# Merged slots for the mixer's gelu-gate and short-convolution columns and for the up projection

## The reference, cut to what matters

```
def hybrid_mixer(u, ...):                       # in each of 2 layers, after a SwiGLU part, before another
    proj = u @ w_in                             # 1024 -> 14 x 1024
    xa, ya, q, k, v, g, sb, sc, sh, gates = jnp.split(proj, cuts, axis=-1)
    xa = causal_depthwise_conv(xa, lru_conv_w) + lru_conv_b
    ha = rg_lru(xa, ...)                        # a gated linear recurrence over the tokens
    oa = (ha * jax.nn.gelu(ya)) @ w_lru_out
    ...
    oc = (sb * causal_depthwise_conv(sc * sh, sc_conv_w)) @ w_sc_out
    ga, gb, gc = jnp.split(jax.nn.sigmoid(gates), 3, axis=-1)
    return (ga * oa + gb * ob + gc * oc) @ w_out

def second_block(...):
    ...
    a = jax.nn.relu(v_ @ w_up)                  # 1024 -> 4096
    ff = (a * a) @ w_down                       # 4096 -> 1024
```

## Time and profile before

| | us |
|---|---|
| median of 3 runs | 2032.05 (2031.1 to 2034.25) |
| the profiled execution | 2034.39 |
| its span | 2032.2 |
| TensorE busy | 1994.3 (98%) |
| VectorE busy | 1299.5 (64%) |
| ScalarE busy | 983.2 (48%) |

### The profile page before, as it was taken

The page is one execution under the profiler, slowest core; times in us unless marked ns, Lnnn a source line. Parts: engine busy times, 40 slices in busy tenths (PEclk is TensorE's granted clock), DMA queues, the critical chain, the costliest instruction groups (busy, mean ns, idle before and its releaser), DMA issues.

```text
span 2032.2 us, 27980 instructions
## 1 busy us (share of the span) xinstructions
PE 1994.3 (98%) x11612; PEld 1748.8 (86%) x11612; DVE 1299.5 (64%) x1601; ACT 983.2 (48%) x1358; POOL 102.9 (5%) x211
## 2 busy tenths in 40 slices
PE   9999999999999999999999999999999999999996
PEld 7888998879898888888889987888888888889985
DVE  7656777546556674766569754465667566766555
ACT  5445465354434544544455644543454445754443
POOL 1003000000000000100300000000010001010000
PEclk9999999999999999999999999999999999999999
DMA  7656456535656556565554464455655656345661
GB/s 252 203 186 212 131 187 202 192 125 167 205 188 207 166 187 201 172 206 187 191 193 165 150 224 149 163 186 187 207 168 187 228 184 194 119 156 188 186 208 61
DMA packets 245148, 369.31 MB, mean 182 GB/s; under 512 B 6679, under 2 KB 180023, under 8 KB 245022
## 3 DMA queue, kind: packets, MB, share of 16 engines
q1 hardware_dynamic: 240000, 352.34, 52.7%
q0 software_dynamic: 4528, 14.85, 2.2%
q10 hardware_dynamic: 494, 0.32, 0.1%
HBM read 366.28 MB, written 1.08 MB: 181 GB/s over the span
## 4 chain that ended last, share of the span: by engine, by line
PE 89%; DVE 5%; ACT 2%; DMA 1%; issue 1%; POOL 1%; DVEq 0%; SPq 0%; POOLq 0%; ACTq 0%
PE ps L1741 19%; PE ps L1551 19%; PE ps L1534 14%; PE ps L1535 7%; PE ps L1522 6%; PE ps L1524 6%; PE ps L1523 6%; PE ps L1612 4%; PE ps L1576 1%; DMA raw<-in_ffn_w_in_dram 1%; DVE w_lo L1016 1%; PE ps L1685 1%; DVE u L1066 1%; DVE a L1171 1%; PE ps L1896 1%
## 5 line engine op out<-in xcount | busy, mean ns | idle before, releaser
L1016 DVE TENSOR_TENSOR w_lo<-raw,w_hi 128x1024 fp32r<-128x1024 f32 (+1 forms) x658 | 765.5, 1207 | 366.5 <-ACT w_hi L658 364.7
L658 ACT ACTIVATE w_hi<-raw 128x1024 fp32r<-128x1024 f32 (+1 forms) x658 | 653.1, 1042 | 392.3 <-PE ps L1551 196.1
L1534 PE MATMUL ps<-u,w_hi 128*128 128x512 f32 x1280 | 451.1, 397 | 0.3 <-DVE act L1125 0.3
L1535 PE MATMUL ps<-u,w_lo 128*128 128x256 f32 x1280 | 359.2, 281 | 0.0
L1522 PE MATMUL ps<-u,w_hi 128*128 128x256 f32 x1072 | 306.5, 286 | 0.1
L1524 PE MATMUL ps<-u,w_lo 128*128 128x256 f32 x1072 | 303.3, 283 | 0.0
L1523 PE MATMUL ps<-u,w_hi 128*128 128x256 f32 x1072 | 303.3, 283 | 0.0
L1534 PEld LDWEIGHTS ps<-u,w_hi 128*128 128x128 f32 x1280 | 240.2, 188 | 59.0 <-issue 0.8
L1535 PEld LDWEIGHTS ps<-u,w_lo 128*128 128x128 f32 x1280 | 241.8, 189 | 0.2
L1741 PE MATMUL ps<-w_hi,u 128*128 128x512 f32 x640 | 205.4, 396 | 2.0 <-DVE w_lo L1016 2.0
L1522 PEld LDWEIGHTS ps<-u,w_hi 128*128 128x128 f32 x1072 | 205.6, 192 | 1.4 <-issue 0.8
(11 more groups left out here) (279 smaller groups left out, 2517.0 us busy)
## 6 DMA issues: line engine op xcount, KB each, us to landing
raw<-in_w_mix_in_dram SPq DMA_DIRECT2D x112, 1024.0 KB, 5.1
raw<-in_ffn_w_in_dram SPq DMA_DIRECT2D x88, 1024.0 KB, 5.1
raw<-in_ffn_w_out_dram SPq DMA_DIRECT2D x40, 1024.0 KB, 4.9
raw<-in_w_ret_out_dram SPq DMA_DIRECT2D x16, 1024.0 KB, 5.0
raw<-in_w_up_dram SPq DMA_DIRECT2D x16, 1024.0 KB, 5.5
raw<-in_w_down_dram SPq DMA_DIRECT2D x16, 1024.0 KB, 4.9
raw<-in_w_in_dram SPq DMA_DIRECT2D x9, 1024.0 KB, 5.3
raw<-in_w_lru_out_dram SPq DMA_DIRECT2D x8, 1024.0 KB, 5.0
```

Source lines behind the costliest of these rows:

```text
L658: A(parts(n)[0][:, part], raw[i % RAW][:, part], ACT.Copy).then_inc(heads_done, 1)
L1016: V.tensor_tensor(parts(n)[1][:, part], raw[i % RAW][:, part], parts(n)[0][:, part], ALU.subtract)\
L1534: M(ps[:, bank0 + a, :], hi[:, k, c], u[:, :, k, :], start=k == 0, stop=False)
L1535: ins = M(ps[:, bank0 + a, 0:S], lo[:, k, c], u_hi[:, k, :], start=False, stop=k == KD - 1)
```

## The change

The column slots of ya, sc, sh and sb in both layers and those of the up projection (but not its head slots) become wide slots. Each then fills two banks: bank pair (2+2j) mod 4 in the mixer, 2(p mod 2) in the up projection, so two results can wait instead of four. ScalarE copies the half with `hi*lo` into an SBUF tile, and VectorE adds the half from PSUM to it. What used the bank now uses the sum. For ya there is one tile for the sum, `act2[:, 1]`, so ScalarE copies ya j only after Gelu of ya j-1. In the up projection Relu is no longer taken by ScalarE; VectorE's square becomes max(x, 0) * x. TensorE waits for the add (`col_summed`, `relu_summed`) where it waited for the reader of the bank. The two head slots of the up projection are turned back into banks 4 and 5 instead of 1 and 2.

```diff
+WIDE = ("ya", "sc", "sh", "sb")
...
+        def col_halves(j):
+            return wide_halves((2 + 2 * j) % 4)
+        def col_sum(j):
+            return act2[:, j % 2, :].rearrange("p (a n) -> p a n", a=2)
... ScalarE, mixer
                         elif name == "ya":
-                            A(tiles(a2)[:, pair, :], pv, ACT.Gelu_apprx_tanh).then_inc(gelu_ready.sem, 1)
+                            if j >= 1:
+                                act.wait_ge(gelu_ready.sem, gelu_ready.at(l, j))
+                            A(col_sum(1), col_halves(j)[1], ACT.Copy).then_inc(col_low.sem, 1)
+                            act.wait_ge(col_summed.sem, col_summed.at(l, col_index(name, j) + 1))
+                            A(tiles(a2)[:, pair, :], col_sum(1), ACT.Gelu_apprx_tanh).then_inc(gelu_ready.sem, 1)
...
                         elif name == "sc":
-                            A(tiles(a1)[:, pair, :], pv, ACT.Copy).then_inc(sc_ready.sem, 1)
+                            A(tiles(a1)[:, pair, :], col_halves(j)[1], ACT.Copy).then_inc(col_low.sem, 1)
+                        elif name in ("sh", "sb"):
+                            if j >= 2:
+                                used = sh_ready if name == "sh" else oc_ready
+                                act.wait_ge(used.sem, used.at(l, j - 1))
+                            A(col_sum(j), col_halves(j)[1], ACT.Copy).then_inc(col_low.sem, 1)
... ScalarE, up projection
-                        A(act2[:, p % 2, :], ps[:, (9 + p) % 4, :], ACT.Relu).then_inc(b["relu_ready"], 1)
+                        if p < 2:
+                            A(act2[:, p % 2, :], ps[:, 4 + p, :], ACT.Copy).then_inc(b["relu_low"], 1)
+                        else:
+                            A(act2[:, p % 2, :].rearrange("p (a n) -> p a n", a=2), wide_halves(2 * (p % 2))[1], ACT.Copy)\
+                             .then_inc(b["relu_low"], 1)
... VectorE, mixer, after ahead(n) and ahead of the recurrence
+                        if name in WIDE:
+                            i = col_index(name, j)
+                            part = tiles(a1)[:, pair, :] if name == "sc" else col_sum(1 if name == "ya" else j)
+                            dve.wait_ge(col_low.sem, col_low.at(l, i + 1))
+                            V.tensor_tensor(part, col_halves(j)[0], part, ALU.add).then_inc(col_summed.sem, 1)
...
-                            V.tensor_tensor(prod_pad[:, pair, 2:2 + S], pv, tiles(a1)[:, pair, :], ALU.mult)\
+                            V.tensor_tensor(prod_pad[:, pair, 2:2 + S], col_sum(j), tiles(a1)[:, pair, :], ALU.mult)\
...
-                            own.done(V.tensor_tensor(tiles(a1)[:, pair, :], pv, tiles(a1)[:, pair, :], ALU.mult))
+                            own.done(V.tensor_tensor(tiles(a1)[:, pair, :], col_sum(j), tiles(a1)[:, pair, :], ALU.mult))
... VectorE, up projection
-                        V.tensor_tensor(mul2[:, p % 2, :], act2[:, p % 2, :], act2[:, p % 2, :], ALU.mult)\
-                         .then_inc(b["sq_ready"], 1)
+                        if p < 2:
+                            dve.sem_inc(b["relu_summed"], 1)
+                        else:
+                            low = act2[:, p % 2, :].rearrange("p (a n) -> p a n", a=2)
+                            V.tensor_tensor(low, wide_halves(2 * (p % 2))[0], low, ALU.add).then_inc(b["relu_summed"], 1)
+                            dve.wait_ge(b["relu_summed"], p + 1)
+                        V.scalar_tensor_tensor(mul2[:, p % 2, :], act2[:, p % 2, :], 0.0, act2[:, p % 2, :], ALU.max,
+                                               ALU.mult).then_inc(b["sq_ready"], 1)
... TensorE, mixer
-                            if name == "sc":
-                                pe.wait_ge(g_ready.sem, g_ready.at(l, j + 5))
+                            if name in WIDE and j >= 2:
+                                emptied_columns(l, name, j - 2)
+                            elif name in WIDE and BEFORE[name] in WIDE:
+                                emptied_columns(l, BEFORE[name], j + 2)
+                            elif name == "sc":
+                                pe.wait_ge(g_ready.sem, g_ready.at(l, 2 * j + 6))
+                            elif name in WIDE:
+                                before = EMPTIED[BEFORE[name]]
+                                pe.wait_ge(before.sem, before.at(l, 2 * j + 2))
...
-                            column_slot(n, bank((2 + j) % 4), u_hi, u_lo)
+                            if name in WIDE:
+                                wide_slot(n, (2 + 2 * j) % 4)
+                            else:
+                                column_slot(n, bank((2 + j) % 4), u_hi, u_lo)
... TensorE, up projection
-                    if p >= 4:
-                        pe.wait_ge(b["relu_ready"], p - 3)
                     if n not in HEADSLOT:
-                        column_slot(n, bank((9 + p) % 4), u_hi, u_lo)
+                        if p >= 4:
+                            pe.wait_ge(b["relu_summed"], p - 1)
+                        wide_slot(n, 2 * (p % 2))
                     if p == 2:
-                        turn_back(G_UP, (1, 2))
+                        turn_back(G_UP, (4, 5))
```

More of the change, by code:

```diff
@@ L272, in half_view, with col_index @@
             return [a.rearrange("p (k n) -> p k n", n=512) for a in parts(n)]
+        def col_index(name, j):
+            return 4 * WIDE.index(name) + j
+        def col_halves(j):
+            return wide_halves((2 + 2 * j) % 4)
+        def col_sum(j):
+            return act2[:, j % 2, :].rearrange("p (a n) -> p a n", a=2)
         def half_bank(e, tt):
@@ L346, in build @@
         ret_ready = signal("ret_ready", HEADS, 1)
-        sc_ready = signal("sc_ready", 4)
+        col_low = signal("col_low", 4 * len(WIDE))
+        col_summed = signal("col_summed", 4 * len(WIDE))
         sh_ready = signal("sh_ready", 4)
@@ L369, in build @@
             "attn_rows", "attn_sum", "attn_scale", "attn_scaled", "o_turned", "o_head", "o_ready",
-            "relu_ready", "sq_ready", "hid_ready", "p_loaded",
+            "relu_low", "relu_summed", "sq_ready", "hid_ready", "p_loaded",
             "p_turned", "p_head", "p_ready", "brow_loaded", "gate_rows", "gate_in", "gate_ready", "gated", "ple_sum",
@@ L825, in mixer @@
                         ahead(n)
-                        if name in ("xa", "ya", "sc") or name in ("ga", "g", "gb", "gc") and j % 2 == 1:
+                        if name in ("xa", "ya", "sc", "sh", "sb") or name in ("ga", "g", "gb", "gc") and j % 2 == 1:
                             emptied(n)
@@ L1289, in mixer @@
                         elif name == "sb":
-                            dve.wait_ge(slot_used, n + 1)
-                            own.done(V.tensor_tensor(tiles(a1)[:, pair, :], pv, tiles(a1)[:, pair, :], ALU.mult))
+                            dve.wait_ge(col_summed.sem, col_summed.at(l, i + 1))
+                            own.done(V.tensor_tensor(tiles(a1)[:, pair, :], col_sum(j), tiles(a1)[:, pair, :], ALU.mult))
                             split(tiles(a1)[:, pair, :], h_hi[:, pair, :], h_lo[:, pair, :], oc_ready.sem)
@@ L1447, in _ @@
                         p = 8 * part + j
[L1448 to L1450 removed]
+                        dve.wait_ge(b["relu_low"], p + 1)
+                        if p < 2:
[6 more added lines that the diff above has]
+                                               ALU.mult).then_inc(b["sq_ready"], 1)
                         dve.wait_ge(b["sq_ready"], p + 1)
@@ L1723, in turn_head, with emptied_columns @@
                 ins.then_inc(ret_turned.sem, 1)
[L1726 to L1729, removed]
+            EMPTIED = {"xa": xa_ready, "q": q_ready, "k": k_ready, "ga": ga_ready, "lru_out": acc_ready,
+                       "gb": gb_ready, "ret_out": ret_added, "gc": gc_ready}
+            BEFORE = {"q": "xa", "k": "q", "ya": "k", "ga": "ya", "lru_out": "ga", "g": "lru_out", "sc": "g",
                       "sh": "sc", "gb": "sh", "ret_out": "gb", "sb": "ret_out", "gc": "sb", "sc_out": "gc"}
+            def emptied_columns(l, name, j):
+                pe.wait_ge(col_summed.sem, col_summed.at(l, col_index(name, j) + 1))
             def half_slot(n, k0, act_hi, act_lo, e, first, last):
@@ L1762, in row_form @@
                     else:
-                        before = EMPTIED[BEFORE[name]]
-                        pe.wait_ge(before.sem, before.at(l, 2 * e + 2))
+                        if BEFORE[name] in WIDE:
+                            emptied_columns(l, BEFORE[name], 2 + e)
+                        else:
+                            before = EMPTIED[BEFORE[name]]
+                            pe.wait_ge(before.sem, before.at(l, 2 * e + 2))
                 if name == "lru_out" and j == 0:
@@ L1992, in _ @@
                     if n == B_DN2 + 4:
-                        pe.wait_ge(b["relu_ready"], 16)
+                        pe.wait_ge(b["relu_summed"], 16)
                         pe.wait_ge(b["p_loaded"], 16)
```

3 lines of the change are left out of this document (1 added, 2 removed).

## The result

| | us |
|---|---|
| the changed kernel, median of 8 runs | 2037.89 (2036.90 to 2039.18) |
| the kernel before, median of 8 runs | 2032.90 (2031.10 to 2034.25) |
| ratio, with its 95% interval | 1.0023 [1.0013, 1.0034] |
| the profiled execution and its span | 2036.92, 2035.1 |

It is slower, by 4.7 us (2.6 to 6.9, by the ratio). The forecast was 2036.4, and +4.3.

The account below looks back on a forecast made before the run. TensorE, computing 98% of the span, was taken as the bound. Slips at ya of +9.3 us less 5.0 saved in merged slots gave +4.3, median 2032.05 to 2036.4; range 2033.4 to 2039.8.

Parts of the forecast that it names:

- The slip at ya: ya0 to ya3: ScalarE's copies, loads and waits for adds delay recurrence and ga1 by 4.67 us a layer, +9.3 together.
- One small wait: At ya3, TensorE waiting for the sum of ya1 (302.74 against 302.72) costs nothing, since slot 18 waits anyway.
- The load has no drain: ScalarE's table loads at ya: 1.28 us uncovered, without the skill page's 1.38 drain, which would add 2.8.
- No slack behind 310.34: VectorE from the first layer's recurrence start: no pause, so any delay there delays ga1 at 337.20 equally.
- The gain elsewhere: 38 merged slots in sc, sh, sb and up save 5.0 us; 1.5 by the skill page's figures.
- all nineteen quick: sc1 to sh3 in both layers and up 3 to 7 all at quick pace: 1.9 us beyond 4.1.
- Nothing elsewhere: sc, sh, sb and up: copies and adds make TensorE wait nowhere; cover 1.2 us at gb2, 0.4 at up's entry.
- The sum: Whole kernel: +9.3 - 5.0 = +4.3 us, median 2032.05 becomes 2036.4.
- The forecast's edge of 4.06 us: Whole kernel: 0.2%, about what a measurement can tell from none; slower by more than that had chance 0.51.
- A: All 38 merged slots outside ya: quick pace everywhere, 7.8 us gained, +1.5, 2033.6; chance 0.12.
- B: ya0 to ya3: the recurrence doesn't slip, ScalarE's added waits lie in time it has, -5.0, 2027.1; chance 0.06.
- C: sh or the entry of up: VectorE falls behind by more than 1.2 us of cover, +7.3, 2039.4; chance 0.15.

Follow-up runs that it names:

- experiment 1: Changed kernel with ya put back to column slots, Gelu straight from the bank; sc, sh, sb and up stay merged: 2028.72 us, 0.9968 of the kernel before.
- experiment 2: Kernel before with only ya merged into wide slots: 2044.25 us, 1.0041 of the kernel before.
- experiment 5: Changed kernel plus a one-column Gelu ahead of the wait for ya0, to preload Gelu's table: 2036.49 us, 1.0011 of the kernel before.
- experiment 6: Changed kernel with VectorE's add of ya3 moved behind the first recurrence step: 2041.47 us, 1.0035 of the kernel before.
- experiment 3: Changed kernel with Exp and Sqrt ahead of all Gelus, each Gelu one slot later, ya3's add behind the first recurrence step: 2025.60 us, 0.9952 of before.
- experiment 4: Changed kernel with ya in column slots, Exp and Sqrt ahead of all Gelus, each Gelu one slot later: 2026.91 us, 0.9958 of the kernel before.
- experiment 7: Changed kernel with eight small matmuls, results overwritten, ahead of sb0 in both layers and of the second up half: 2042.91 us, one run.

## Why the prediction was right, point by point

- **The slip at ya.** Right, step by step. On the clock of before the forecast had the Gelu of ya0 at 293.54, the head of slot 15 at 298.67, that of 16 at 303.23, that of 17 at 311.06 and the recurrence at 315.01. The profile after has, with 1.86 added, 293.45, 298.61, 303.22, 311.06 and 315.01. ga1 was to slip 4.67 a layer and slipped 4.68 and 4.67; the waits were to be "some 12 us" and are 10.6. By start times the eight waits cost 12.7. Experiments 1 and 2 put all of it on ya, 5 and 6 show that it is a queue's order and not the table load alone. One small wait was put at nothing and did show: TensorE starts ya3 0.26 late, for the sum of ya1. As the prediction said, the waits behind it swallow it: in experiment 5 it is gone, and the slip is still 4.1.
- **The load has no drain.** Load and function start 1.29 apart here too (290.30, 291.59). The term that ScalarE: Activation LUTs, in the Trainium skill, section What ACT_TABLE_LOAD costs, would have added is not seen.
- **No slack behind 310.34.** Right for later starts: what came late there came out at ga1. Experiments 3 and 4 show the other direction, which the forecast didn't price: a start 1.85 earlier shortened the stretch by 1.31, and one 3.6 earlier by 1.33. That is the wait of before by start times, and with it gone an earlier recurrence is worth nothing.
- **The gain elsewhere.** The step "I take half of that: gain 5.0" was too low. It is the one term of the sum that was mis-sized. In the profile after all nineteen slots behind a turn were quick: 2.01 in each mixer (135.28 less 133.27) and 2.01 in up, together 6.03, where all nineteen quick had been reckoned at 4.1 + 1.9. The half came from two quick runs behind a turn "and not in a third"; the trace of before has four such runs, two quick (thirteen slots from 683.80, seven from 1518.87) and two slow (from 35.64 and from 872.07), so that the evidence was even. Of these the fourteen in sc and sh were quick in every profile of merged ones, the five of up in five of seven (5.668 in experiments 5 and 7). The figures of TensorE: Matmul & The Clock Gate, in the Trainium skill, section Back-to-back issue gap, by which the gain was estimated at 1.5, are off by four times here.
- **Nothing elsewhere.** Right. The first half of gb2's split was to be done 1.3 ahead of TensorE: it is done at 516.82 (the splits start at 515.60, 1.22 each), and gb2 starts at 518.17 (507.27 and two row slots of 5.45). At the entry of up the add of p2 ends at 1834.19 and TensorE takes p4 at 1834.53, a cover of 0.34 where 0.4 was forecast.
- **The sum.** 9.36 less 6.03 is +3.3, a microsecond under the forecast's +4.3, and that microsecond is the gain. The spans differ by 2.9, because the stretches that weren't changed differ too: -1.86 up to ya, and +1.37 in the second feed-forward part. The timed difference, +4.7 (2.6 to 6.9), holds both +3.3 and +4.3, so the times alone don't check the sum to a microsecond. That the medians lie +5.0 apart, within 0.7 of the forecast, is partly luck: the gain was put 1.0 too low, and the 1.7 between +3.3 and +5.0 is in no stretch that changed; one run of unchanged slots can move the time by 1.37. The rest of the miss is that the median of before went from 2032.05 to 2032.90 with more runs. The forecast's edge of 4.06 us lies inside the interval too, so on which side of it the change fell is not settled.
- **Rivals.** A (quick everywhere): sb and the second up half stayed at 5.65 in every run (5.67 and 5.66 behind the small matmuls). B (no slip): the slip is there; but experiments 3 and 4 are B made true, by another order, at -9.8 and -8.5. C (VectorE behind in sh): no wait at gb2.

## What to carry to other kernels

A saving on the engine that bounds a kernel counts only where that engine doesn't already wait; first look at which queue its last wait comes from, and whether the new helper work (a copy, a wait for an add, a table load) enters that queue ahead of the instruction that the wait is for. Here 6.0 us were won on TensorE in 38 slots and 9.4 lost in ScalarE's order at eight, and another order of the same work, with two table loads a layer less, won the loss back and a wait of the old kernel too. In a kernel like this one, try a result's last step behind the next slot's weight preparation where it has to wait for another engine (experiment 6 shows what one such wait ahead of it costs), and group functions that share a table.

## What the runs showed of the hardware

A merged pair (512 and 256 moving columns) has two paces, 5.65 and 5.55 us per 16 pairs, 353 and 347 ns a pair. The granted clock is 1.00, the 2.4 GHz level, in both (684 to 756 before, quick; 1900 to 1945 in the profile after, slow). The quick pace is what the other forms' spacings add up to, an estimate from their rows: 5.45 / 24 = 0.227 for 512 columns and 5.759 / 48 = 0.120 for 256. The slow one has 6 ns more a pair.

A run keeps its pace from its second or third slot to its end, and which one it is changes between executions of the same instructions. In the first feed-forward part, where nothing was changed, thirteen slots took 5.697 us each in the profile before, 5.599 in the one after and 5.659 in experiment 4. These are averages with the first slots in them: before it is 6.12, 5.75 and then 5.65; after, 6.12, 5.66 and then 5.55; in experiment 4, 5.73 and then 5.65. The thirteen of the second feed-forward part went at 5.659 in the profile after (684.60 to 758.17) and at 5.554 before.

One such run moves the time by 1.37 us, and there are three. That could be a good part of the spread of one kernel's times, but with one profile of each kernel it is not shown. What picks the pace stays open. Every run straight behind row slots was slow. Behind the transposes of a turn, sc1 to sh3 were always quick and the feed-forward runs now and then. Small matmuls ahead of a run did not bring the quick pace (experiment 7). But transposes aren't needed for it: ya, when merged, follows four matmuls of the recurrence's gates, and ya1 took 5.55 in every profile that has it. In experiment 5, from ya1 to ya3, two slots:

```profile
291.08 0.39 PE L1574 MATMUL ps<-u,w_hi 128*128 128x512 f32 x1
...
302.18 0.39 PE L1574 MATMUL ps<-u,w_hi 128*128 128x512 f32 x1
```
